# Second block's first mixer: a bank order of its own, one convolution a step, gates two steps and cells one step later

## What is computed

```python
p = h @ w_in
qk = silu(causal_conv(p[..., :2 * W], conv_w))       # W = 768: 16 tiles of 96 channels, 4 taps
v, o = p[..., 2 * W:3 * W], p[..., 3 * W:4 * W]
gates = p[..., 4 * W:4 * W + 8] + gate_bias           # input and forget gate of 4 heads
cell = mlstm_chunkwise(q, k, v, i_gate, f_gate)       # cumsum of log_sigmoid(f), running max, exp weights
cell = rms_norm(cell, h_gain)
h_a = sigmoid(o) * cell
h_m = memory_cross_attention(q_mem, mem_n, ...)
return concat([h_a, h_m]) @ w_out
```

## Time and profile before

| | us |
|---|---|
| three runs, median | 2423.27 (2422.98 to 2424.35) |
| the profiled execution, its own time | 2424.13 |
| its span, first to last instruction | 2422.8 |
| PE busy | 2381.7 (98%) |
| DVE busy | 1646.3 (68%) |
| ACT busy | 1239.8 (51%) |
| mean granted clock of TensorE | 0.996 |

### The profile page before, as it was taken

How to read it: one execution, slowest core, us unless ns; L and a number is a source line. 1 busy time by engine, 2 the same in 40 slices (tenths; PEclk the granted TensorE clock), 3 DMA queues, 4 the chain that set the end, 5 groups by cost and what they waited for, 6 DMA issues and landing times.

```text
span 2422.8 us, 45847 instructions
## 1 busy us (share of the span) xinstructions
PE 2381.7 (98%) x18834; PEld 2288.6 (94%) x18834; DVE 1646.3 (68%) x2919; ACT 1239.8 (51%) x2084; POOL 52.3 (2%) x102
## 2 busy tenths in 40 slices
PE   8999999999999999999999999999999999989999
PEld 7999988999999998899999999889999999978999
DVE  6656877775486568777756875776765767584764
ACT  5444555554464445555544654565544655455542
POOL 2001100000000011000000000000000010000000
PEclk9999999999999999999999999999999999999999
DMA  7654633465556554356655664434665676532763
GB/s 208 177 177 130 162 88 109 127 193 178 174 155 176 178 146 128 89 156 165 185 190 152 194 186 151 125 104 124 192 188 169 169 203 200 163 105 74 208 188 132
DMA packets 588720, 382.79 MB, mean 158 GB/s; under 512 B 44719, under 2 KB 564371, under 8 KB 588512
## 3 DMA queue, kind: packets, MB, share of 16 engines
q1 hardware_dynamic: 585360, 376.77, 53.7%
q0 software_dynamic: 3152, 3.08, 0.5%
HBM read 378.66 MB, written 1.07 MB: 157 GB/s over the span
## 4 chain that ended last, share of the span: by engine, by line
PE 89%; DVE 6%; ACT 2%; issue 1%; DMA 1%; SPq 0%; DVEq 0%; ACTq 0%
PE bank L584 88%; DVE wlo L2004 1%; ACT whi L1327 1%; DVE ry L2023 0%; DVE ry L2021 0%; PE bank L914 0%; DVE ybuf L2054 0%; DVE smh L2438 0%; PE bank L682 0%; DMA wraw<-in_w_ffn_gu 0%; DVE hT L2058 0%; DVE xlo L2037 0%; DMA wraw<-in_ffn_w_gate 0%; DVE ssum L2016 0%; DVE rst L2025 0%
## 5 line engine op out<-in xcount | busy, mean ns | idle before, releaser
L2004 DVE TENSOR_TENSOR wlo<-wraw,whi 128x1024 fp32r<-128x1024 f32 (+2 forms) x723 | 866.2, 1205 | 285.9 <-ACT whi L1327 283.2
L1327 ACT ACTIVATE whi<-wraw 128x1024 fp32r<-128x1024 f32 (+2 forms) x723 | 747.8, 1043 | 591.4 <-DMA wraw<-in_w_ffn_gu 170.6
L584 PE MATMUL bank<-xhi,whi 128*128 128x256 f32 (+3 forms) x3928 | 583.2, 288 | 11.3 <-ACT whi L1327 4.0
L584 PE MATMUL bank<-xhi,wlo 128*128 128x256 f32 (+3 forms) x3928 | 570.5, 285 | 7.2 <-DVE wlo L2004 7.2
L584 PE MATMUL bank<-xlo,whi 128*128 128x256 f32 (+3 forms) x3928 | 560.8, 284 | 0.0
L584 PEld LDWEIGHTS bank<-xhi,whi 128*128 128x128 f32 (+2 forms) x3928 | 514.7, 188 | 30.2 <-issue 9.0
L584 PEld LDWEIGHTS bank<-xhi,wlo 128*128 128x128 f32 (+2 forms) x3928 | 514.5, 188 | 10.6 <-DVE wlo L2004 10.2
L584 PEld LDWEIGHTS bank<-xlo,whi 128*128 128x128 f32 (+2 forms) x3928 | 510.1, 187 | 0.2
L584 PE MATMUL bank<-act_hi,wlo 128*128 128x256 f32 (+1 forms) x1408 | 400.6, 284 | 0.0
L584 PE MATMUL bank<-act_lo,whi 128*128 128x256 f32 (+1 forms) x1408 | 400.4, 284 | 0.0
L584 PE MATMUL bank<-act_hi,whi 128*128 128x256 f32 (+1 forms) x1408 | 398.6, 283 | 0.0
(11 more groups left out here) (408 smaller groups left out, 1830.5 us busy)
## 6 DMA issues: line engine op xcount, KB each, us to landing
wraw<-in_w_ffn_gu SPq DMA_DIRECT2D x176, 512.0 KB, 3.9
wraw<-in_w_ffn_down SPq DMA_DIRECT2D x88, 512.0 KB, 3.2
wraw<-in_ffn_w_gate SPq DMA_DIRECT2D x88, 512.0 KB, 4.0
wraw<-in_ffn_w_up SPq DMA_DIRECT2D x88, 512.0 KB, 3.9
wraw<-in_ffn_w_down SPq DMA_DIRECT2D x88, 512.0 KB, 3.3
wraw<-in_w_in SPq DMA_DIRECT2D x80, 512.0 KB, 3.8
wraw<-in_a_w_in SPq DMA_DIRECT2D x24, 384.0 KB, 3.3
wraw<-in_w_out SPq DMA_DIRECT2D x16, 512.0 KB, 3.8
```

The costliest lines, as they stand in the source:

```text
L584: return E.matmul(out_, lhsT, rhs, start=first, stop=last, skip_group_check=True)
L1327: A.activation(flat(whi, u), flat(wraw, u), ACT.Copy).then_inc(S("hi"), 1)
L2004: V.tensor_tensor(flat(wlo, u), flat(wraw, u), flat(whi, u).bitcast(F32), ALU.subtract).then_inc(lo_ready[u % RING], 1)
```

## The change

Five edits, all for this one stage. The first ten projections after the head's begin get banks by a list: numbers 0 to 5 banks 0 to 5 as before, 6 to 9 banks 0 to 3, later ones 0 and 1 in turn; a projection waits only for the last one in its own bank. The second, third and fourth convolution go from steps 2, 3, 3 to 3, 4, 5. The gates go from steps 2 and 3 to 4 and 5 on DVE, and from steps 2 and 4 to 4 and 6 on ACT. The cells start at 7, 13, 19, 25 instead of 6, 12, 18, 24. PE waits for the evacuation of the tenth projection (`aqk` 10, bank 3) before the first head's broadcast into bank 2. The silus of the first head go with the fourth convolution from step 4 to 6; of the others nothing moves.

```diff
-A_CONV_STEP = [2, 2, 3, 3] + [A_STEP["aqk", i] + 1 for i in A_CONV[4:]]
-A_CELL_STEP = (6, 12, 18, 24)
+A_CONV_STEP = [2, 3, 4, 5] + [A_STEP["aqk", i] + 1 for i in A_CONV[4:]]
+A_CELL_STEP = (7, 13, 19, 25)
+A_BANKS = [i if i < 6 else i - 6 if i < 10 else i % 2 for i in range(len(A_HEAD + A_ORDER))]
@@ bank_of @@
+    STAGE_BANKS = {MIX_FIRST: MIX_BANKS, 6: A_BANKS}
-        if c.banks == MIX_FIRST:
-            return MIX_BANKS[i]
+        if c.banks in STAGE_BANKS:
+            return STAGE_BANKS[c.banks][i]
@@ next_bank on TensorE @@
-            if c.banks == MIX_FIRST:
-                before = [j for j in range(i) if MIX_BANKS[j] == MIX_BANKS[i]]
+            if c.banks in STAGE_BANKS:
+                banks = STAGE_BANKS[c.banks]
+                before = [j for j in range(i) if banks[j] == banks[i]]
                 if before:
                     E.wait_ge(S("evac"), c.first + before[-1] + 1)
@@ cells on TensorE, head 0 @@
                         m.then_inc(S("a_ct"), 1)
+                        E.wait_ge(S("evac"), c.first + 10)
@@ gates on ScalarE and on VectorE @@
-                while c.step < 2:
+                while c.step < 4:
```

## The result

The changed kernel takes 2433.8 us, the median of six runs (2431.8 to 2435.2), against 2423.6 for the kernel before in the same session (six runs, 2423.0 to 2425.3). The ratio is 1.0041, with a 95% interval of 1.0031 to 1.0052, that is 10.2 us slower (7.5 to 12.6). The forecast was 9.1 slower. The profiled execution took 2432.46 against 2424.13.

What follows compares the result with a forecast made beforehand. PE was taken as the bound, its stalls waiting on a full DVE and lowering its clock. Terms 3.1 + 1.4 + 2.5 + 2.1 = 9.1 us on 2423.3 gave 2432.4 us, range 2426.5 to 2436.

Steps and rivals of the forecast that it cites:

- Step 7: First head's broadcast and scores: PE waits for aqk 10's evacuation, then the silus; 3.1 us later, 0.55 if clock holds.
- no drain: Table load before step 7's silus: silu follows without a drain; by the skill's page the sum would be 1.4 larger.
- Steps 22 and 23: Head 2's maximum moves behind a convolution and the first norm, delaying PE's mean square: 1.4 us, between 0.9 and 1.5.
- Step 26: First memory score waits for head 3's products behind mkv 3's take and a norm: 2.5 us, plus 2.1 for the clock.
- the waits that I called hidden: Heads 0 and 1, steps 10/11 and 16/17: 2.8 us of work hidden behind a projection of 2.87.
- no PE wait hangs on the norm that ACT's silus delay: Heads 0 and 1: DVE's norm waits for ACT's ln and exp, but no PE wait depends on it within two steps.
- a wait for DVE leaves the clock alone: Rival: stalls on DVE never cost the clock, step 7 costs 0.55, time 2427.8 us; chance 0.07.
- only step 7 counts: Rival: the later meetings at steps 22, 23 and 26 find cover, time 2426.4 us; chance 0.10.
- The other side: Rival at step 7: evacuation and silus are done when PE arrives; 2421 us, or 2417.4 with later costs hidden; chance 0.05.

Runs made afterwards that it cites:

- e3: Changed kernel with projection 8 in bank 4, projection 9 in bank 1, and PE's new wait for the tenth evacuation removed: 2432.3 us, ratio 1.0044.
- e4: Changed kernel with the first four convolutions back at steps 2, 2, 3, 3: 2429.2 us, ratio 1.0028.
- e1: Kernel before with only the cells' steps moved to 7, 13, 19, 25: 2430.6 us, ratio 1.0033.
- e8: Changed kernel with DVE's third and fourth norm behind the cells of their step, the first two still ahead: 2429.1 us, ratio 1.0023.
- e5: Changed kernel with the gates back at steps 2 and 3 (2 and 4 on ACT): 2429.4 us, ratio 1.0028.
- e2: Changed kernel with all of DVE's cells ahead of the norms within a step: 2434.2 us, ratio 1.0052.
- e11: Kernel before with aqk 3 in bank 4, changed low-part leads, ACT's first copies and silus earlier, aqk 10's low part behind av 1's take: 2419.1 us, ratio 0.9987.
- e7: Kernel before with projection 8 in bank 4 and DVE's low parts three instead of four slabs ahead in steps 3 to 5: 2419.5 us, ratio 0.9991.
- e6: Kernel before with one edit, projection 8 (aqk 3) in bank 4: 2422.2 us, ratio 1.0002.

## Why the prediction was right

**Step 7, predicted 3.1, measured 1.7.** The mechanism came out piece by piece: the idle spot of DVE (1.21 us, I had 1.8), PE's stall before `av` 1 (0.39, I had 0.4), the evacuation of `aqk` 10 as one end and the silus behind the tap of `aqk` 3 as the other (e3, e4). The replay of the queues put the scores at 1542.9, which is 37.9 us into the stage; they began at 37.2. The gap of 0.6 is the smaller idle spot: the high parts started 0.6 us earlier than I held them to. The rest of the miss is the clock. I took 5.1 us of slow work behind the restart, as before; the stretch was again 6.8 us, but it began during the wait, and only some 3.8 us of it lay behind the start of the scores. The table load fits the replay as well: the silu starts 0.01 us behind its end (1538.64 + 1.28, then 1539.93), so it was right to add no drain.

**Steps 22 and 23, predicted 1.4, measured 1.3.** Stall 0.98 before the norm matmul, where I had 0.9; the mean square behind it hardly waited.

**Step 26, predicted 2.5 and 2.1 for the clock, measured 5.9.** The stall is 2.48, by the releaser I named (e1, e8). The clock did fall, as taken, but for 6.8 us, of which nearly all was work: 3.4 us, my upper bound, and not the 2.1 that I took. This term was the mis-sized one in this profile; by luck it made up for step 7. It is also a matter of the draw: e1, e3, e4 and e5 have the same stall (2.47 or 2.48 us) with 3.4 us at half clock behind it, and e1's place costs 4.3 us instead of 5.9; at step 7 e2 and e8 have the changed kernel's stalls with 10.2 us at half clock. That the stage came out within 0.2 us of the sum is therefore luck in the clock's lengths. What the runs bear out is the stalls, their places and who ends them.

**No later cost or gift.** The last milestone and the stage's end have the same distance, 8.9, so heads 0 and 1 and the waits that I called hidden were hidden. One remark in the prediction holds for its kernel and no further: that no PE wait hangs on the norm that ACT's silus delay. In e2 one did.

**The rivals.** That a wait for DVE leaves the clock alone is out; both long stalls that DVE ended (4.67 and 2.48) have half clock with them, and in e8, where the second is 0.70, the clock stays full. The Trainium skill (TensorE: Matmul & The Clock Gate, "Loop structure matters more than you think") has DVE's copy out of PSUM not break PE's warmth, in a loop whose next matmuls follow at once. Here they did not follow at once, and the trace shows what a PE that stands for DVE pays; the page's loop itself no run here tests. A stall of 2.46 us was followed by full clock in the kernel before, one of 2.48 us was not here. That only step 7 counts is out by e1. The other side, the bank order that wins, did not come in this kernel; e11, with bank 4 alone and not this list, shows what an early `aqk` 3 needs, and I had named the point rightly (evacuation and silus in time) while taking the silus' place as given. The time lies 1.4 us above the forecast, while the stage's 8.9 is 0.2 below it; the profiled execution differs by 8.3. The repeated runs of one kernel spread over 3.4 us, and the clock of other stages has stretches that come and go, so I don't explain this 1.4.

## What to carry to other kernels

A PE stall that ends with an evacuation is a question about the evacuating engine's list: if that engine is full, another bank only moves the stall, and what paid here (3.0 and 3.5 us of stage in e7 and e11, a tenth of a per cent of the time) was to put the take, the copy or the activation that releases PE ahead of work that nobody waits for yet. When a pipeline of side work is moved by one step, go through every step at which it meets another side, since the list within a step decides who waits; here two such meetings cost more than the place that the change was about. Price the clock with the stall, and by the work that follows it: in e6 the half clock took back all that an earlier start had won, and in e4 nearly half of it. And before a difference of one or two us is put down to an edit, compare the lengths at half clock in both profiles.

## What was unexpected of the hardware

Apart from those that the end of a profile cuts off, the stretches at half clock have few lengths: 3.4 us and 6.8 us, each several times over the fourteen profiles, and 10.2 us in four places (at step 7 in e2, e3 and e8, and in e1's last mixer). The same stall can be followed by the one or the other: 3.65 us before `aqk` 3 by 6.8 in the kernel before and 3.4 in e1 (means 0.66 in the earlier trace rows and 0.83 here).

```profile
1530.00:1540.00 10.00, 6.57 (x43) 6.57 (x44) 6.90 (x13) 6.43 (x10) 0.00 (x0) 0.83 0.25 62
```

By the end of `mkv` 2 this pair differs by 0.7 us (41.5 and 40.8), since before part of the stretch lay in the stall; at step 26, where all of it is work, 6.8 instead of 3.4 us costs 1.6 (5.9 and 4.3). That is about as much as the smaller effects looked for here. The runs don't show what sets the length.
